# A two-feed-forward residual block on one core: feed-forwards in three parts, with shared units in the down pairs too

## What is computed

```python
h = h + 0.5 * swiglu(rms_norm(h, ffn1_norm[i]), ffn1_w_gate[i], ffn1_w_up[i], ffn1_w_down[i])
u = rms_norm(h, mix_norm[i])
...                                  # u @ w_in, attention, linear attention, merge gates
h = h + merged @ w_out[i]
h = h + 0.5 * swiglu(rms_norm(h, ffn2_norm[i]), ffn2_w_gate[i], ffn2_w_up[i], ffn2_w_down[i])
ple_gate = sigmoid(rms_norm(h, ple_norm[i]) @ w_ple_gate[i])
h = h + ple_gate * (p[i] @ w_ple_proj[i])
out = rms_norm(h, final_norm)

def swiglu(x, w_gate, w_up, w_down):
    return (silu(x @ w_gate) * (x @ w_up)) @ w_down      # 2048 -> 5632 -> 2048
```

## Time and profile before

| | |
|---|---|
| median of three runs | 2218.12 us (2217.25 to 2218.17) |
| the profiled execution's own time | 2217.39 us |
| its span, first to last instruction | 2215.3 us |
| TensorE busy | 2202.3 us (99%), 9899 matmuls |
| VectorE busy | 1409.5 us (64%), 1432 instructions |
| ScalarE busy | 1073.8 us (48%), 1183 instructions |
| granted TensorE clock | 0.999 |
| DMA | 425.68 MB, 192 GB/s in the mean |

### The profile page before, as it was taken

How to read it: one execution, slowest core, us unless ns; L and a number is a source line. 1 busy time by engine, 2 the same in 40 slices (tenths; PEclk the granted TensorE clock), 3 DMA queues, 4 the chain that set the end, 5 groups by cost and what they waited for, 6 DMA issues and landing times.

```text
span 2215.3 us, 24399 instructions
## 1 busy us (share of the span) xinstructions
PE 2202.3 (99%) x9899; PEld 1817.2 (82%) x9899; DVE 1409.5 (64%) x1432; ACT 1073.8 (48%) x1183; POOL 39.4 (2%) x71
## 2 busy tenths in 40 slices
PE   9999999999999999999999999999999999999998
PEld 7888888888888888877777888888888888888886
DVE  5988645688755544445655665788864568875555
ACT  6545443454544444454444545464543346444454
POOL 0000000000010000010010000000000000000000
PEclk9999999999999999999999999999999999999999
DMA  8655555654555666655555665655546665556664
GB/s 288 239 176 193 179 190 186 233 214 173 190 179 187 200 193 195 180 174 169 175 170 161 186 186 180 232 205 180 201 171 190 190 237 200 186 182 198 190 190 143
DMA packets 165705, 425.68 MB, mean 192 GB/s; under 512 B 11592, under 2 KB 11600, under 8 KB 150368
## 3 DMA queue, kind: packets, MB, share of 16 engines
q1 hardware_dynamic: 163840, 419.21, 58.1%
q0 software_dynamic: 1472, 4.70, 0.8%
q10 hardware_dynamic: 288, 0.30, 0.0%
HBM read 422.06 MB, written 2.11 MB: 191 GB/s over the span
## 4 chain that ended last, share of the span: by engine, by line
PE 98%; DMA 1%; issue 0%; DVE 0%; ACT 0%; ACTq 0%; POOLq 0%; POOL 0%
PE acc L1493 18%; PE acc L1495 18%; PE acc L1494 18%; PE acc L1536 6%; PE acc L1538 6%; PE acc L1537 6%; PE turn L1538 4%; PE turn L1536 4%; PE turn L1537 4%; PE fox L1538 4%; PE fox L1537 4%; PE fox L1536 4%; PE turn L1513 1%; DMA raw<-in_ffn_up 0%; PE acc L1530 0%; PE turn L1787 0%
## 5 line engine op out<-in xcount | busy, mean ns | idle before, releaser
L1025 DVE TENSOR_TENSOR w_lo<-raw,w_hi 128x1024 fp32r<-128x1024 f32 x451 | 558.0, 1240 | 585.1 <-ACT w_hi L594 584.6
L594 ACT ACTIVATE w_hi<-raw 128x1024 fp32r<-128x1024 f32 x451 | 477.1, 1060 | 682.9 <-PE acc L1495 643.0
L1493 PE MATMUL acc<-w_hi,x_both 128*128 128x512 f32 x940 | 371.0, 395 | 0.8 <-DVE x_both L1188 0.8
L1495 PE MATMUL acc<-w_hi,x_both 128*128 128x512 f32 x940 | 366.6, 390 | 0.0
L1494 PE MATMUL acc<-w_lo,x_both 128*128 128x512 f32 x940 | 366.3, 390 | 0.0
L1493 PE MATMUL acc<-w_hi,slab_r 128*128 128x512 f32 x832 | 325.5, 391 | 0.0
L1495 PE MATMUL acc<-w_hi,slab_r 128*128 128x512 f32 x832 | 324.2, 390 | 0.0
L1494 PE MATMUL acc<-w_lo,slab_r 128*128 128x512 f32 x832 | 324.0, 389 | 0.0
L1493 PEld LDWEIGHTS acc<-w_hi,x_both 128*128 128x128 f32 x940 | 176.6, 188 | 42.5 <-issue 5.7
L1495 PEld LDWEIGHTS acc<-w_hi,x_both 128*128 128x128 f32 x940 | 176.5, 188 | 37.4
L1494 PEld LDWEIGHTS acc<-w_lo,x_both 128*128 128x128 f32 x940 | 176.7, 188 | 35.2
(11 more groups left out here) (432 smaller groups left out, 3513.6 us busy)
## 6 DMA issues: line engine op xcount, KB each, us to landing
raw<-in_ffn_w_down SPq DMA_DIRECT2D x176, 512.0 KB
raw<-in_ffn_up SPq DMA_DIRECT2D x50, 1024.0 KB, 4.9
raw<-in_w_in SPq DMA_DIRECT2D x96, 512.0 KB
lo_raw<-in_ffn_up SPq DMA_DIRECT2D x42, 1024.0 KB, 4.9
raw<-in_w_merge_gate SPq DMA_DIRECT2D x64, 512.0 KB
more<-in_ffn_up SPq DMA_DIRECT2D x25, 1024.0 KB, 4.9
raw<-in_ffn_up SPq DMA_DIRECT2D x33, 512.0 KB, 3.9
raw<-in_w_out SPq DMA_DIRECT2D x32, 512.0 KB
```

What stands on the lines that cost most here:

```text
L594: nc.scalar.activation(w_hi[:, slot, :, :], raw[:, slot, :, :], ACT.Copy).then_inc(hi_split, 1)
L1025: nc.vector.tensor_tensor(w_lo[:, slot, :, :], raw[:, slot, :, :], w_hi[:, slot, :, :].bitcast(F32), ALU.subtract).then_inc(lo_split, 1)
L1493: nc.tensor.matmul(to, hi(kt)[:, tok], w_hi[:, slot, k, :], start=kt == 0, stop=False)
L1495: last = nc.tensor.matmul(to, lo(kt)[:, tok], w_hi[:, slot, k, :], start=False, stop=kt == BK * nb - 1)
```

## The change

Each feed-forward now has three parts of 4, 4 and 3 up pairs (`PARTS`), and the down projection of a part is two down pairs with four banks of 512 columns, like an up pair. Up and down pairs stand in one list of 17 (`PAIR`, places 0 to 16: up 0 to 3, down 4 and 5, up 6 to 9, down 10 and 11, up 12 to 14, down 15 and 16), each a stage. A down pair has 8, 8 or 6 units and two shared ones (`HS`). Only the first pair of a feed-forward has none (in the first feed-forward the first two). That is 9 + 10 up pairs with three and 6 + 6 down pairs with two, 81 shared units.

A stage is now `B S B S B S A A A S S`: the B and the plain units by turns, and the A before the last two plain units. ACT's silu and VectorE's `hidden_out` come at the second item, the transposes after the third, and `turn_hidden` of ACT and VectorE after the fifth (the fourth in stages of eight items). Where the pair before is a down pair, VectorE adds its four banks to `h` at the second item instead. The sums of activations for the shared down units are made from an extra unrounded copy (`hid_full`), which ACT makes when it takes back the transposes of the first up pair of a part. In the first stage of a feed-forward the sums for the up pairs come one item earlier. Trios go to whichever was freed first. The last stage of each feed-forward finishes column group by column group. `p` is now turned just ahead of the first rows of the last down pair. The masks and thin weights of the mixing phase are made and loaded after the feed-forward instead of before its last down projection.

The diff, cut to its core:

```diff
-HALF_KT = (24, 20)
+PARTS = (4, 4, 3)
...
-US = 3
+US, HS = 3, 2
...
-def stage_of(pair, first, pairs):
-
-    own = [("S", pair, u) for u in range(UNITS)]
-    if pair > first:
-        own = [("B", pair, u) for u in range(US)] + own[US:]
-    if pair + 1 < pairs:
-        own = [*own[:-1], *[("A", pair + 1, u) for u in range(US)], own[-1]]
+def shared_units(ffn, i):
+
+    if i <= FIRST[ffn] or i >= PAIRS:
+        return 0
+    return US if PAIR[i].kind == "up" else HS
...
+def stage_of(ffn, i):
+
+    b, a = shared_units(ffn, i), shared_units(ffn, i + 1)
+    plain = [("S", i, u) for u in range(b, PAIR[i].units)]
+    own = []
+    for u in range(b):
+        own.append(("B", i, u))
+        if len(plain) > 2:
+            own.append(plain.pop(0))
+    own += plain
+    if a:
+        own = [*own[:-2], *[("A", i + 1, u) for u in range(a)], *own[-2:]]
     return own
...
+def sum_made_at(i):
+    return 4 if PAIR[i].part == len(PARTS) - 1 else 2
+
+
+def turned_at(stage):
+    return 4 if len(stage) >= 10 else 3
...
+                    held = [trio_of[pair, n] for n in range(u)]
+                    trio = min((t for t in range(US) if t not in held),
+                               key=lambda t: trio_free[t])
...
@@ scalar
+            def turn_hidden(name, pair):
+                for ct in range(2):
+                    t = UP_TURN[name] + 2 * PAIR[pair].n + ct
+                    act.wait_ge(turned, t + 1 - TURNS["x"])
+                    kt, bank = PAIR[pair].kt0 + 2 * ct, banks_of(name, pair)[2 * ct][:, :].rearrange("p (k c) -> p k c", k=2)
+                    if kt < BK * HS:
+                        nc.scalar.activation(hid_full[:, kt // BK, :, :], bank, ACT.Copy)
+                    nc.scalar.activation(slab_r[:, kt:kt + 2, :], bank, ACT.Copy).then_inc(turned_hi, 1)
...
@@ vector, for each item k of stage i
                         if k + 1 < len(stage) and stage[k + 1].kind == "A":
                             make_steps(name, stage[k + 1])
                         split_item(name, it)
...
+                        if k == 0 and shared_units(name, i):
+                            combine(name, i)
+                        if k == 1 and i > 0 and PAIR[i - 1].kind == "up":
+                            hidden_out(name, i - 1)
+                        if k == 1 and i > 0 and PAIR[i - 1].kind == "down":
+                            dve.wait_ge(multiplied, stage[0].at)
+                            for ct in range(2):
+                                add_rows(2 * PAIR[i - 1].n + ct, banks_of(name, i - 1)[2 * ct:2 * ct + 2], 0.5)
                         if k == 1 and n == 0 and later_rows:
                             later_rows()
-                        if 3 <= k <= 5 and n == 0 and sums is not None:
-                            split_sums(k - 3, sums)
-                        if 2 <= k <= 4 and n == 0 and sums is not None:
-                            make_sums(k - 2, hi, lo, sums)
-                        if k == hidden_at(n) + 3 and pair > 0:
-                            turn_hidden(name, pair - 1, kts)
+                        if n == 0 and 2 <= k <= 4:
+                            split_sums(name, i + 1, k - 2)
+                        if n == 0 and 1 <= k <= 3:
+                            make_sums(name, i + 1, k - 1, hi, lo)
+                        if k == turned_at(stage) and i > 0 and PAIR[i - 1].kind == "up":
+                            turn_hidden(name, i - 1)
+                        if i + 1 in LAST_UP and k == sum_made_at(i):
+                            make_sums(name, i + 2, 0)
+                        if i + 1 in LAST_UP and k == sum_made_at(i) + 1:
+                            split_sums(name, i + 2, 0)
...
@@ tensor
+                        if k == 2 and hidden_turned:
+                            turn_hidden(name, i - 1)
+                        if i == PAIRS - 1 and k == 1:
+                            if p_turn:
+                                pe.wait_ge(read_out, ROWS[down_turn] + 1)
+                                pe.wait_ge(tail_full, 16)
+                                turn(TURN["p"], TURN["p"] % 2, lambda k, tok: p_tm[:, tok, k * P:(k + 1) * P])
+                            turn_rows(down_turn, 0)
```

More of the change, by code:

```diff
@@ L69, in hidden_at, with ffn_pairs @@
[L69 to L77, removed]
+HID = 16
+NEXT_OF = {"ffn1": "project", "ffn2": "ple"}
+FIRST = {"ffn1": 1, "ffn2": 0}
+Pair = namedtuple("Pair", "kind part n units kt0")
+def ffn_pairs():
+    pairs, j = [], 0
+    for part, ups in enumerate(PARTS):
+        kt0 = 4 * sum(PARTS[:part])
+        pairs += [Pair("up", part, j + n, UNITS, 4 * n) for n in range(ups)]
+        pairs += [Pair("down", part, n, 2 * ups, kt0) for n in range(2)]
+        j += ups
+    return pairs
@@ new lines @@
+PAIR = ffn_pairs()
+PAIRS = len(PAIR)
+LAST_UP = [i for i in range(PAIRS - 1) if PAIR[i].kind == "up" and PAIR[i + 1].kind == "down"]
+def shared_units(ffn, i):
+    if i <= FIRST[ffn] or i >= PAIRS:
+        return 0
+    return US if PAIR[i].kind == "up" else HS
+Item = namedtuple("Item", "kind pair unit at quad quad_free raw raw_free raw_split raw_count trio trio_free trio_count step")
+def stage_of(ffn, i):
[9 more added lines that the diff above has]
+        own = [*own[:-2], *[("A", i + 1, u) for u in range(a)], *own[-2:]]
+    return own
@@ L425, in feed_forward @@
[L425 to L429 removed]
+                            sp.dma_start(to[:, 0:3:2, :], first).then_inc(tall_full[it.raw], 16)
+                            if it.trio_free > 0:
+                                sp.wait_ge(multiplied, it.trio_free)
+                            sp.dma_start(later_tiles(name, it.trio, 0)[0][:, 0:2, :], second).then_inc(trio_full[it.trio], 16)
@@ L1187, in x_part @@
+                        if i == PAIRS - 1 and k == 5:
+                            turn_rows("down" + name[-1], 1, next_hi, next_lo, gain)
+                dve.wait_ge(half_done, 1 if name == "ffn1" else 2)
+                add_rows(2, banks_of(name, PAIRS - 1)[0:2], 0.5)
             def x_part(kt):
@@ L1545, in multiply_item @@
                 t0, t1 = slice(0, P), slice(P, TOK)
-                pe.wait_ge(lo_split, it.at + 1)
-                if it.kind == "S":
-                    for ct in range(2):
-                        ready(ct)
-                        for k in range(BK):
-                            for t, tok in enumerate((t0, t1)):
-                                last = product(banks[2 * ct + t][:, :], hi(first + k)[:, tok], lo(first + k)[:, tok],
-                                               whole[:, 2 * k + ct, :], rest[2 * k + ct],
-                                               not primed and it.unit == 0 and k == 0, not primed and last_unit and k == 1, primed)
@@ L1569, in tiles_of, with feed_forward @@
+                for n, (x, x_rest, bank) in enumerate(of_tokens):
+                    last = product(banks[bank][:, :], x, x_rest, whole[:, n, :], rest[n], begin, end, it.kind == "B")
+                return last
             def tiles_of(first_turn):
                 return lambda j: pe.wait_ge(turned_lo, first_turn + j + 1)
-            def up_groups(name, hi, lo, sums=None, first_rows=None):
-                pairs, first = UPS[name]
+            hidden_of = of(slab_r, slab_r, 0, HID)
+            def feed_forward(name, x_pair, first_rows=None, p_turn=False):
+                down_turn = "down" + name[-1]
```

562 lines of the change are left out of this document (285 added, 277 removed).

## The result

| | before | after |
|---|---|---|
| median of seven runs | 2218.12 us | 2225.40 us (2223.92 to 2227.33) |
| ratio | | 1.0035, 95% interval 1.0024 to 1.0046 |
| the profiled execution's own time | 2217.39 us | 2224.44 us |

The change makes the kernel 0.35% slower. The forecast was 2224.7 us.

The account below looks back on a forecast made before the run. TensorE's matmuls, their number times their distance, were taken to bound the kernel. 2217.4 - 20.4 saved + 27.0 of new waits = 2224.0 us profiled, 2224.7 for the median; range 2214.5 to 2234.

Parts of the forecast that it names:

- What is taken away: On TensorE: 30 more shared units, each with 3 matmuls fewer, 90 x 0.2267 = 20.4 us off.
- Slip = end of the split - due time + 0.19: Rule for TensorE's loss when VectorE's split is late, from one traced case; nothing gives it back later.
- P: Start of a stage's transposes; VectorE free at P + 2.47, second A due at P + 16.52, slip 0.81 us.
- The load: Third A's trio, free only after the third B: its lone half lands after 3.9 us; slip 1.07 or 1.08.
- The extra copies: First up pair of a part: ScalarE's four copies free VectorE 0.88 us later, at P + 3.35; slip 1.69, three times.
- Place 13: Both feed-forwards: extra copies, sums and their split fall between transposes and second A; 3.7 us each, 7.4 together.
- The first feed-forward's first stage: Sums one item earlier were to make TensorE wait 0.3 us, as its wait for the silu starts earlier.
- Places 3, 4, 5, 9, 10, 11, 14, 16, `combine` and POOL's queue: Stages, combining and mixing-phase masks and thin loads, all claimed to add no wait: costed at nothing.
- The cover holds: Rival, chance 0.12: TensorE hides VectorE's work in every shared stage; the whole 20.4 us is gained, time 2197.7.
- The lone loads are slow: Rival, chance 0.13: lone trio loads land after 5.45 us, adding 15.2 us of waits; time 2239.9.
- Gain eaten, no more: Rival, chance 0.30: waits sum to only 16 to 25 us; with loads landing in 2.5 us, time 2219.9.

Follow-up runs that it names:

- run 6: Changed kernel with A ahead of only the last plain unit; first-stage sums, last down pair's first rows and taking back of transposes each one item later: 2197.32 us.
- Runs 2 and 3: Each against the changed kernel. 2: transposes taken back one item later, 2218.38 us. 3: third B ahead of the second plain unit, 2218.89 us.
- run 1: Changed kernel with the A one item later, ahead of only the last plain unit: 2203.39 us.
- run 4: Changed kernel with no shared units for down pairs, and without their sums and extra copies: 2233.05 us.
- run 8: Changed kernel with the A one item earlier, ahead of the last three plain units: 2340.58 us, one run.
- run 7: Changed kernel with transposes taken back one item later and the third B ahead of the second plain unit: 2207.41 us.

## Why the prediction was right

**What is taken away** was right: the four edits of run 6 bring out 20.1 us by the medians of one chip (20.3 by the profiled executions, 19.9 by their spans), where the step had 20.4. The distance in this kernel stayed at 0.2267 us. The isolated distance of 215.8 ns by the Trainium skill (TensorE: Matmul & The Clock Gate, Back-to-back issue gap) would have made 19.4, and the trace does not agree with it.

**Slip = end of the split - due time + 0.19**, a rule taken from one case, held: with the ends and due times of the changed kernel's trace it gives all 19 losses to L1153 within 0.02 us. The new waits are 26.0 us where 27.0 was forecast. That the total came within 1 us as well is in part luck: the 1.2 of the start and the 0.6 unexplained, neither of them forecast, stand against the 1.0 too much. The part that did the work is the comparison of two clocks from the same event P: 14.67 us of VectorE behind P + 2.47 against 14.05 of TensorE. A busy share of 71% says nothing of it.

**The load.** 3.9 was taken for the lone half; 4.0 was seen in place 6. Runs 2 and 3 show where it decides: alone in 6 and 12, as the last of two in 2 and 8. The estimate of 3.2 us, from the fit that the page DMA: Bandwidth & Descriptors of the Trainium skill (Anatomy of one DMA) gives for loads from GpSimd's queue, would have left places 6 and 12 with a slip of 0.4; they had 1.03 to 1.18, so the trace does not agree with it for loads that SP issues. (The prediction says that by it the load would never decide; by its own sum it still would in 6 and 12, and the waits would be 3.8 us fewer, not 3.5.)

**The extra copies** were right, and the due time beside them was not: VectorE was free at P + 3.34 for 3.35 and its split ended at P + 18.01 for 18.02, but the second A was due at P + 16.63 to 16.65 for 16.52. So places 7 and 1 lost 1.55 to 1.58 for 1.69. **Place 13** was the term most off: 3.7 for 3.4, and as one wait where there are two. I followed VectorE only to the second A, and missed that the plain unit ahead of it was already late by 1.26. Both lie in the sum by which the second A was late, so the total barely changed; but it matters for a cure, since putting the A later alone leaves 0.4 there (run 1). **The first feed-forward's first stage** was to wait 0.3 and did not.

**Places 3, 4, 5, 9, 10, 11, 14, 16, `combine` and POOL's queue** were costed at nothing, and no wait is there.

**The rivals.** "The cover holds" was wrong as a description of this order, but right on what it would be worth: 2197.7 was its price, and 2197.3 is what the kernel takes once the cover is there. "The lone loads are slow" is out: in places 2, 6, 8 and 12 the third steps began 3.9 to 4.0 us after the issue, and one load of 5.7, in run 4, did what this rival says. "Gain eaten, no more" is out by 5.5 us at its price of 2219.9, by the loads it had landing in 2.5 (of places 2 and 8 it took off 0.5, where its own VectorE slip of 0.81 takes off 1.0); but 26.0 us of waits are only 1 above its upper end.

**Open.** The last 0.6 us between the two spans, and why a load of 512 KB now and then takes 5.7 us or more, were not followed.

## What to carry to other kernels

Work moved off a full engine pays only as far as the engine that prepares it stays ahead *at each place*; take one event both engines share, add up what each has to do from there to the same item, and compare, whatever the busy shares say. When two causes stand one behind the other (here VectorE's own queue and a load, in places 1 and 7), each cure alone gave 7.0 and 6.5 us, both together 18.0, and one more item of distance 22.0; so look at what is late next before judging an edit. Ask the order first: here one plain unit behind the A or ahead of it is 22 us, more than the whole saving.

## What was not expected of the hardware

A long wait can cost more than its length. In the feed-forwards of the other runs, whose waits were up to 2.2 us and once 3.0 between two starts (run 4), the matmuls behind them soon kept 0.227 us again. In run 8 15 waits, with 3.1 to 5.5 us between two matmuls' starts, were followed by 5 to 12 matmuls 0.427 us apart at a granted clock of 0.50, and the 24 others, with 1.2 to 2.4 us, were not. The length alone does not decide: in the first 20 us of the profiled executions, 3.52 us between two starts in run 2 (at 12.55) went with a granted clock of 0.50, and 3.24 us in run 7 (at 12.28) with 1.00. The Trainium skill (TensorE: Matmul & The Clock Gate, Wait — 56ns, not 53.3ns?) gives 426.7 ns for 512 columns at the lower level, and the trace agrees; for the upper level it gives 215.7, and the trace has 226.7 throughout.
